# Mask additions spread between scalings, and the end of attention reordered in pairs, in a one-core two-block transformer kernel

## The chip, the cores and the metric

The kernel runs on one core of a Trainium2 chip. The metric is the device time of one execution in microseconds; the median of several runs is compared.

## What is computed

Two small transformer blocks run one after the other on 272 tokens (16 meta tokens and 256 others) of width 1024, in float32. The part that the change touches first is sparse attention in the first block. An index score chooses at most 64 keys for each query; the others are masked, and each head's logits get a bias:

```python
score = jnp.einsum('bqhs,bqh->bqs', jax.nn.relu(s_idx), wb)
top_val, top_idx = lax.top_k(score, n_sel)            # n_sel = 64
logits = jnp.einsum('bqhc,bqkc->bhqk', q_lat, c_sel) * ATT_HEAD_DIM ** -0.5
logits = logits + jnp.moveaxis(bias, -1, 1)           # one bias per head
p = jax.nn.softmax(logits, axis=-1)
u = jnp.einsum('bhqk,bqkc->bqhc', p, c_sel)
...
h = h + dsa_mixer(hn, ...)
h = h + swiglu(rmsnorm(h, norm_ffn[i]), ...)
```

The second block has latent attention (`mla_mixer`) in the same place of its second layer, followed by the same kind of residual addition, norm and gated feed-forward.

## The kernel before

All activations stand transposed in SBUF: `h[:, k, :]` is channel chunk k of 8 (128 channels on the partitions, 272 tokens along the row). Every float32 matrix product is made from three reduced-precision products: an operand is split into a high part (made by ScalarE: `uh` for weights, `xh` or `ah` for activations) and a rest (made by VectorE: `ul`, `xl`, `al`, each the value minus its high part). TensorE then multiplies high by high, high by rest and rest by high: 24 matmuls for a weight unit of 128 output channels (`product`, L489 to L491).

The weights come in slabs of 1 MB into 3 buffers `raw`. SyncE starts the load of slab s when the high parts and rests of slab s-3 are made. A slab gives two units. The calls `hi()` on ScalarE (L949) and `lo()` on VectorE (L1431) convert the next unit wherever they stand in the written order: `hi()` runs up to five units ahead of TensorE and `lo()` up to four. Each engine runs its instructions in the written order; semaphores tie the engines together. There are 4 PSUM banks for the linear products (`lin`) and 4 for the rest (`aux`), used in turn: a bank is filled again only when its last reader has signalled.

**The sparse attention's loop** runs over steps t. In step t TensorE multiplies the query unit of head t (t < 8) or a part of the output projection (`rows`, L531 to L533); then, for t-5, it multiplies the turned weights with the values (`attended`, L719), for t-4 it turns the normalised weights (`weights_turned`, L708: two transposes for the first 128 queries, three for the others), and for t-2 it makes the logits (`dsa_logits`, L697). VectorE in step t converts a unit (`lo()`), inverts the sums of head t-4 (L1773), copies a part of the turned weights (L1702), adds the masked bias to the logits of head t-3 (L1786), takes the two maxima (L1789), negates them (L1792) and scales the queries of head t out of PSUM (L1799). ScalarE takes the exponentials of head t-3 (L1233). GpSimd multiplies the exponentials of a head with the inverted sums, in two instructions (L2135); TensorE's transposes wait for them through `s_dp`.

The mask, once VectorE has made it (`d_acc`, L1769), is added to the biases of the 8 heads by GpSimd (L2129, 128x416 each, signal `s_bm`); L1786 for head hd waits for `s_bm` of hd+1. GpSimd makes all eight additions and then begins to scale.

**The end of both attentions** (`rows_h`, stages "d" and "m"). The output projection leaves its sums in four banks, two channel chunks a bank; the last matmul of bank j is of L533. For each chunk k VectorE adds the bank's half to `h` (L1467), ScalarE makes `xh` from it (L955) and VectorE then `xl` (L1437). TensorE needs `xh` and `xl` of chunk k in the k-th triple of matmuls of the feed-forward's first unit (unit 0, L489 to L491). GpSimd sums the squares of the chunks in `squares`: for k < 6 it squares (L2080) and adds (L2088); for k = 6, 7 VectorE squares (L1471), in `rows_h`, and GpSimd only adds. TensorE sums over the partitions after unit 1 (`total`, L555), ScalarE takes the root (L978), VectorE inverts it (L1447) and scales the finished banks (`gate`, L1443), by which bank 0 comes free for unit 4. Of the three `lo()` in `rows_h`, the first makes the rest of the feed-forward's unit 0, the second that of unit 1 and the third that of unit 2. The `hi()` ahead of the root on ScalarE is that of unit 6, whose slab is loaded into the buffer that unit 0 and 1 leave.

Of the kernel before, what the change touches and what calls it, by code (L numbers as in the profile page):

```python
# [9 lines left out]
ALU = mybir.AluOpType  # L10
# [4 lines left out]
T = 272  # L15
NM = 16
TQ = 256
D = 1024
KC = 8
# [83 lines left out]
def build(nc, A, out):  # L103
    ctx = ExitStack()
    with ctx:
        def sb(name, shape, dt=F32):
            return ctx.enter_context(nc.sbuf_tensor(name, shape, dt))

        def sem(name):
            return ctx.enter_context(nc.semaphore(name))  # L110

        h = sb("h", [P, KC, T])
# [16 lines left out]
        sqt = sb("sqt", [P, 2, T])  # L129
# [260 lines left out]
        def unit_hi(u):  # L390
            n = unit_n(u)
            return uh[u % NFIRST][:, 0:n * P].rearrange("p (k n) -> p k n", k=n)

        def unit_lo(u):
            n = unit_n(u)
            return ul[u % NUNIT][:, 0:n * P].rearrange("p (k n) -> p k n", k=n)

        def pieces(u):

            s, view, kc = units[u]  # L400
            src = view(raw[s % NRAW])
            if kc == "pad":
                return [(src, slice(0, src.shape[2]))]
            if kc == "heads":
                return [(src[:, g], slice(32 * g, 32 * g + 32)) for g in range(4)]
            return [(src, slice(0, P))]
# [8 lines left out]
        lin = Banks(psum[0:4], s_mm, {"D": sem("s_lin_dve"), "A": sem("s_lin_act"), "do": s_dout, "mo": s_mout})  # L415
# [11 lines left out]
        s_xh, s_xl, s_sq, s_ssq, s_rbc = (  # L427
            [sem(f"{n}{i}") for i in range(9)] for n in ("s_xh", "s_xl", "s_sq", "s_ssq", "s_rbc"))
# [988 lines left out]
        def _(e):  # L1417
            w = Seen(e)
# [3 lines left out]
            def lo():  # L1422

                nonlocal u
                if u == NU:
                    return
                w.wait_ge(s_hi, u + 1)
                if u >= NUNIT:
                    w.wait_ge(s_mm, unit_end[u - NUNIT])
                for a, cols in pieces(u):  # L1430
                    i = e.tensor_tensor(unit_lo(u)[:, :, cols], a, unit_hi(u)[:, :, cols].bitcast(F32), ALU.subtract)  # L1431
                i.then_inc(s_lo, 1)
                u += 1

            def x_lo(i, k, n0, g):
                w.wait_ge(s_xh[i], k + 1)
                e.scalar_tensor_tensor(xl[:, k, n0:T], h[:, k, n0:T], g, xh[:, k, n0:T].bitcast(F32), ALU.mult,  # L1437
                                       ALU.subtract).then_inc(s_xl[i], 1)
# [20 lines left out]

            def rows_h(stage, s_done, i, g):  # L1460
                lo()
                for k in range(KC):
                    if k:
                        x_lo(i, k - 1, NM, g(k - 1))
                    half = lin.bank((stage, "sum", k // 2))[:, (k % 2) * TQ:(k % 2) * TQ + TQ]
                    w.wait_ge(*lin.full((stage, "sum", k // 2)))
                    e.tensor_tensor(h[:, k, NM:T], h[:, k, NM:T], half, ALU.add).then_inc(s_done, 1)  # L1467
                    if k >= 6:
                        w.wait_ge(s_done, k + 1)
                        w.wait_ge(s_ssq[i], 2 * k - 3)  # L1470
                        e.tensor_tensor(sqt[:, k % 2, 0:TQ], h[:, k, NM:T], h[:, k, NM:T], ALU.mult).then_inc(s_sq[i], 1)  # L1471
                x_lo(i, KC - 1, NM, g(KC - 1))
                lo()
                lo()

            def wide(stage, parts, i, n0, x0, sq0, g, also=None):
# [284 lines left out]
            for t in range(14):  # L1761
# [8 lines left out]
                hd = t - 4  # L1770
# [7 lines left out]
                hd = t - 3  # L1778
# [15 lines left out]
                if t < 8:  # L1794
                    key = ("dq", t)
                    w.wait_ge(*lin.full(key))
                    if t >= 3:
                        w.wait_ge(*aux.full(("dL", t - 3)))
                    e.scalar_tensor_tensor(d_q[t % 3], lin.bank(key)[:, 0:TQ], 128.0 ** -0.5, rbc[:, NM:T], ALU.mult,  # L1799
                                           ALU.mult).then_inc(lin.empties(key, "D"), 1)  # L1800
            rows_h("d", s_dout, 3, lambda k: G(gcol["norm_ffn"] + 8 + k))

            def meta_square(t):
# [84 lines left out]
            for s in range(32):  # L1888
                hd, r = s // 8, s % 8
# [110 lines left out]
            for a in range(2):  # L2000
# [5 lines left out]
                for m, op in ((0, ALU.subtract), (2, ALU.add)):  # L2006
                    w.wait_ge(*lin.emptied(("mr", a, m // 2)))
                    for g in range(4):
                        rows_ = slice(32 * g, 32 * g + 32)
                        to = slice(64 * (g % 2) + 16 * m, 64 * (g % 2) + 16 * m + 32)  # L2010
                        i = e.tensor_tensor(m_qr[to, 2 * a + g // 2, :], tmp[m][rows_, 0:TQ], tmp[m + 1][rows_, 0:TQ], op)
                    i.then_inc(s_qr, 1)
            for t in range(13):
                lo()
                hd = t - 3
# [7 lines left out]
                hd = t - 2  # L2023
                if 0 <= hd < 8:
# [4 lines left out]
                    for b in range(2):  # L2029
# [4 lines left out]
                    e.tensor_scalar(m_stat[:, 1, 2 * hd:2 * hd + 2], m_stat[:, 0, 2 * hd:2 * hd + 2], -(192.0 ** -0.5),  # L2034
                                    None, ALU.mult).then_inc(s_mmax, 1)
            rows_h("m", s_mout, 7, lambda k: G(gcol["norm_ffn_g_2"] + 8 + k))


# [16 lines left out]
        def _(e):  # L2055
            w = Seen(e)

            def pad(u):

                if u >= NFIRST:  # L2060
                    w.wait_ge(s_mm, unit_end[u - NUNIT])
                e.memset(uh[u % NFIRST][:, :].bitcast(F32), 0.0).then_inc(s_pad, 1)
                e.memset(ul[u % NUNIT][:, :].bitcast(F32), 0.0).then_inc(s_pad, 1)

            def squares(i, stage, n0, between=None):

                total = ssq[0][:, 0:T - n0]
                w.wait_ge(*aux.full(("n", i - 1)))
                for k in range(KC):
                    src, sq = h[:, k, n0:T], sqt[:, k % 2, 0:T - n0]  # L2070
                    if k == 6 and between is not None:
                        pad(between)
                    if k < 6:
                        if stage in ("d", "m"):
                            w.wait_ge(s_dout if stage == "d" else s_mout, k + 1)
                        else:
                            w.wait_ge(*lin.emptied((stage, "o", k)))
                        if i == 4 and k >= 3:
                            w.wait_ge(s_both, k - 1)
                        e.tensor_tensor(sq if k else total, src, src, ALU.mult).then_inc(s_ssq[i], 1)  # L2080
                        w.wait_ge(s_ssq[i], 2 * k)
                    else:
                        w.wait_ge(s_sq[i], k - 5)
                        w.wait_ge(s_ssq[i], k + 5)
                    if i == 4 and k == 1:
                        w.wait_ge(s_both, 1)
                    if k:
                        e.tensor_tensor(total, total, sq, ALU.add).then_inc(s_ssq[i], 1)  # L2088
# [36 lines left out]
            e.tensor_tensor(total, total, sqt[:, 0, :], ALU.add).then_inc(s_dcs, 1)  # L2125
            w.wait_ge(s_bias, 16 * 2 * (P // NR))
            w.wait_ge(s_mask, 1)
            for hd in range(8):
                e.tensor_tensor(d_bias[:, hd, :], d_bias[:, hd, :], d_acc, ALU.add).then_inc(s_bm, 1)  # L2129
            for hd in range(8):  # L2130
                E = d_E[hd % 5]
                w.wait_ge(s_drc, hd + 1)
                for b in range(2):
                    Eb = E[:, KEYS[b]]
                    e.tensor_scalar(Eb, Eb, d_stat[:, 3, 2 * hd + b:2 * hd + b + 1], None, ALU.mult).then_inc(s_dp, 1)  # L2135
            squares(3, "d", NM)


# [177 lines left out]
```

## Time and profile before

| | |
|---|---|
| median of 3 runs | 1436.95 us (1436.87 to 1436.99) |
| the profiled execution's own time | 1435.41 us |
| its span, first to last instruction | 1433.5 us |
| TensorE busy | 1394.1 us, 97% |
| VectorE, ScalarE, GpSimd busy | 954.0, 691.2 and 275.5 us |
| mean granted TensorE clock | 0.991 of full speed |

All rows are of the one profiled execution. PE is TensorE (PEld its weight loads), DVE VectorE, ACT ScalarE, POOL GpSimd, SP SyncE. A matmul's recorded length includes its way through the array, so that back-to-back matmuls overlap in the records.

### The profile page before, as it was taken

The numbers are of one execution on the slowest core, as the hardware profiler recorded it, in microseconds if no ns is written. First come the engines' busy times: TensorE is split into PE (matmuls) and PEld (weight loads), VectorE is DVE, ScalarE is ACT, GpSimd is POOL, SyncE is SP. The second block draws the span as 40 slices with busy tenths as digits, with TensorE's granted clock in tenths as the row PEclk, the third lists the DMA queues.
The fourth block names the chain that finished last, engine by engine and source line by source line (L and its number), as shares of the span: only waits on it lengthen the run. The fifth ranks groups of instructions, "written<-read, shape, count | busy, mean of one in ns | idle before, by whom it ended". The sixth has DMA issues, their size and how long they took to land.

```text
span 1433.5 us, 26896 instructions
## 1 busy us (share of the span) xinstructions
PE 1394.1 (97%) x11056; PEld 1372.8 (96%) x11056; DVE 954.0 (67%) x1520; ACT 691.2 (48%) x1117; POOL 275.5 (19%) x273
## 2 busy tenths in 40 slices
PE   7999999999989999999999999999999999899998
PEld 7999999999989999999999999999999999899997
DVE  5668766656875767668566786766557775766653
ACT  5555544444644544444333564544444554544442
POOL 1024100022053000032233553000023302200021
PEclk9999999999999999999999999999999999999999
DMA  7424566555422655554444455555555552365551
GB/s 233 147 89 152 174 186 191 174 192 176 138 99 89 205 174 191 173 192 147 147 149 136 132 167 174 177 176 177 162 168 158 153 176 89 119 205 182 188 182 68
DMA packets 225489, 229.57 MB, mean 160 GB/s; under 512 B 13576, under 2 KB 218632, under 8 KB 225368
## 3 DMA queue, kind: packets, MB, share of 16 engines
q1 hardware_dynamic: 224432, 225.98, 48.9%
q10 hardware_dynamic: 936, 1.87, 0.6%
q8 instruction: 89, 1.46, 0.5%
q14 instruction: 32, 0.26, 0.1%
HBM read 226.51 MB, written 1.33 MB: 159 GB/s over the span
## 4 chain that ended last, share of the span: by engine, by line
PE 87%; DVE 7%; ACT 2%; issue 2%; POOL 2%; DMA 0%; POOLq 0%; DVEq 0%; ACTq 0%
PE ps L489 26%; PE ps L491 25%; PE ps L490 25%; DVE ul L1431 2%; PE ps L719 1%; PE ps L793 1%; PE ps L561 1%; DVE xl L1437 1%; POOL arena L2129 1%; PE ps L531 1%; PE ps L533 1%; PE ps L532 1%; ACT xh L955 1%; PE ps L708 1%; PE ps L555 1%
## 5 line engine op out<-in xcount | busy, mean ns | idle before, releaser
L949 ACT ACTIVATE uh<-raw 128x1024 fp32r<-128x1024 f32 (+4 forms) x455 | 449.1, 994 | 513.5 <-PE ps L491 468.7
L489 PE MATMUL ps<-xh,uh 128*128 128x272 f32 (+1 forms) x2160 | 631.3, 292 | 11.8 <-DVE xl L1437 8.0
L1431 DVE TENSOR_TENSOR ul<-raw,uh 128x1024 fp32r<-128x1024 f32 (+4 forms) x455 | 528.6, 1168 | 159.8 <-PE ps L491 129.8
L491 PE MATMUL ps<-xh,ul 128*128 128x272 f32 (+1 forms) x2160 | 619.9, 287 | 0.0
L490 PE MATMUL ps<-xl,uh 128*128 128x272 f32 (+1 forms) x2160 | 617.9, 286 | 0.0
L489 PEld LDWEIGHTS ps<-xh,uh 128*128 128x128 f32 x2160 | 409.2, 189 | 18.5 <-issue 12.1
L490 PEld LDWEIGHTS ps<-xl,uh 128*128 128x128 f32 x2160 | 408.8, 189 | 1.3
L491 PEld LDWEIGHTS ps<-xh,ul 128*128 128x128 f32 x2160 | 409.0, 189 | 0.0
L489 PE MATMUL ps<-ah,uh 128*128 128x272 f32 (+1 forms) x1104 | 319.7, 290 | 3.0 <-ACT ah L1077 2.7
L491 PE MATMUL ps<-ah,ul 128*128 128x272 f32 (+1 forms) x1104 | 315.1, 285 | 0.0
L490 PE MATMUL ps<-al,uh 128*128 128x272 f32 (+1 forms) x1104 | 314.9, 285 | 0.0
L1443 DVE TENSOR_TENSOR tmp<-ps,rbc 128x272 f32<-128x272 f32 (+1 forms) x224 | 96.6, 433 | 195.4 <-PE ps L491 192.5
L489 PEld LDWEIGHTS ps<-ah,uh 128*128 128x128 f32 x1104 | 208.5, 189 | 3.8 <-ACT ah L1077 2.9
L490 PEld LDWEIGHTS ps<-al,uh 128*128 128x128 f32 x1104 | 208.9, 189 | 0.5
L491 PEld LDWEIGHTS ps<-ah,ul 128*128 128x128 f32 x1104 | 208.5, 189 | 0.0
L2080 POOL TENSOR_TENSOR ssq<-h 128x272 f32<-128x272 f32 (+1 forms) x8 | 10.2, 1279 | 601.6 <-DVE h L1453 578.7
L2080 POOL TENSOR_TENSOR sqt<-h 128x272 f32<-128x272 f32 (+1 forms) x40 | 52.8, 1320 | 114.4 <-DVE h L1453 113.0
L2088 POOL TENSOR_TENSOR ssq<-ssq,sqt 128x272 f32<-128x272 f32 (+1 forms) x56 | 49.7, 888 | 60.5 <-DVE sqt L1458 54.4
L955 ACT ACTIVATE xh<-h,gains 128x272 fp32r<-128x272 f32 (+1 forms) x48 | 24.8, 517 | 65.4 <-DVE h L1453 48.0
L1000 ACT ACTIVATE ah<-tmp 128x272 fp32r<-128x272 f32 (+1 forms) x88 | 36.9, 420 | 12.9 <-DVE tmp L1503 12.9
L1437 DVE SCALAR_TENSOR_TENSOR xl<-h,gains,xh 128x272 fp32r<-128x272 f32 (+1 forms) x48 | 36.0, 751 | 7.7 <-ACT xh L955 6.9
L1503 DVE TENSOR_TENSOR tmp<-tmp 128x272 f32<-128x272 f32 (+1 forms) x88 | 38.1, 433 | 3.0
(253 smaller groups left out, 1168.7 us busy)
## 6 DMA issues: line engine op xcount, KB each, us to landing
raw<-in_ffn_w SPq DMA_DIRECT2D x60, 1024.0 KB, 5.2
raw<-in_ffn_w_in SPq DMA_DIRECT2D x44, 1024.0 KB, 5.2
raw<-in_ret_w_in SPq DMA_DIRECT2D x24, 1024.0 KB, 5.2
raw<-in_ffn_w_out SPq DMA_DIRECT2D x16, 1024.0 KB, 5.0
raw<-in_gla_w_in SPq DMA_DIRECT2D x12, 1024.0 KB, 6.1
raw<-in_ret_w_o SPq DMA_DIRECT2D x8, 1024.0 KB, 5.0
raw<-in_dsa_w_in SPq DMA_DIRECT2D x7, 1024.0 KB, 5.3
raw<-in_ffn_w_out SPq DMA_DIRECT2D x8, 768.0 KB, 4.3
```

What stands on the lines that cost most here:

```text
L489: e.matmul(ps[:, 0:n1 - n0], hi[:, k, :], x.hi[:, k0 + j, n0:n1], start=first and j == 0, stop=False)
L490: e.matmul(ps[:, 0:n1 - n0], hi[:, k, :], x.lo[:, k0 + j, n0:n1], start=False, stop=False)
L491: i = e.matmul(ps[:, 0:n1 - n0], lo[:, k, :], x.hi[:, k0 + j, n0:n1], start=False, stop=last and j == len(ks) - 1)
L949: i = e.activation(unit_hi(u)[:, :, cols], a, ACT.Copy)
L955: e.activation(xh[:, k, n0:T], h[:, k, n0:T], ACT.Copy, scale=g).then_inc(s_xh[i], 1)
L1000: e.activation(ah[:, c, n0:T], tmp[2 * c % 6][:, 0:n], ACT.Copy).then_inc(s_fh, 1)
L1431: i = e.tensor_tensor(unit_lo(u)[:, :, cols], a, unit_hi(u)[:, :, cols].bitcast(F32), ALU.subtract)
L1437: e.scalar_tensor_tensor(xl[:, k, n0:T], h[:, k, n0:T], g, xh[:, k, n0:T].bitcast(F32), ALU.mult, ALU.subtract).then_inc(s_xl[i], 1)
L1443: e.tensor_tensor(dst, lin.bank(key)[:, 0:T - n0], rbc[:, n0:T], ALU.mult).then_inc(lin.empties(key, "D"), 1)
L1503: e.tensor_tensor(t, t, tmp[(2 * c + 1) % 6][:, 0:n], ALU.mult).then_inc(s_prod, 1)
L2080: e.tensor_tensor(sq if k else total, src, src, ALU.mult).then_inc(s_ssq[i], 1)
L2088: e.tensor_tensor(total, total, sq, ALU.add).then_inc(s_ssq[i], 1)
```

## The change

Two reorderings; no arithmetic is added or taken away.

1. GpSimd adds the mask to the biases of heads 0, 1 and 2 first. Then, after it has scaled head hd, it adds the mask for head hd+3 (for hd < 5).
2. In `rows_h`, VectorE waits once a bank, adds both halves to `h`, and then makes both rests `xl`. The squares of chunks 6 and 7 are made after the second `lo()` and not between the additions and rests.

```diff
             def rows_h(stage, s_done, i, g):
                 lo()
-                for k in range(KC):
-                    if k:
-                        x_lo(i, k - 1, NM, g(k - 1))
-                    half = lin.bank((stage, "sum", k // 2))[:, (k % 2) * TQ:(k % 2) * TQ + TQ]
-                    w.wait_ge(*lin.full((stage, "sum", k // 2)))
-                    e.tensor_tensor(h[:, k, NM:T], h[:, k, NM:T], half, ALU.add).then_inc(s_done, 1)
-                    if k >= 6:
-                        w.wait_ge(s_done, k + 1)
-                        w.wait_ge(s_ssq[i], 2 * k - 3)
-                        e.tensor_tensor(sqt[:, k % 2, 0:TQ], h[:, k, NM:T], h[:, k, NM:T], ALU.mult).then_inc(s_sq[i], 1)
-                x_lo(i, KC - 1, NM, g(KC - 1))
+                for j in range(KC // 2):
+                    w.wait_ge(*lin.full((stage, "sum", j)))
+                    for k in (2 * j, 2 * j + 1):
+                        half = lin.bank((stage, "sum", j))[:, (k % 2) * TQ:(k % 2) * TQ + TQ]
+                        e.tensor_tensor(h[:, k, NM:T], h[:, k, NM:T], half, ALU.add).then_inc(s_done, 1)
+                    for k in (2 * j, 2 * j + 1):
+                        x_lo(i, k, NM, g(k))
                 lo()
+                for k in (6, 7):
+                    w.wait_ge(s_done, k + 1)
+                    w.wait_ge(s_ssq[i], 2 * k - 3)
+                    e.tensor_tensor(sqt[:, k % 2, 0:TQ], h[:, k, NM:T], h[:, k, NM:T], ALU.mult).then_inc(s_sq[i], 1)
                 lo()
...
             w.wait_ge(s_mask, 1)
-            for hd in range(8):
+
+            def hide(hd):
                 e.tensor_tensor(d_bias[:, hd, :], d_bias[:, hd, :], d_acc, ALU.add).then_inc(s_bm, 1)
+
+            for hd in range(3):
+                hide(hd)
             for hd in range(8):
                 E = d_E[hd % 5]
                 w.wait_ge(s_drc, hd + 1)
                 for b in range(2):
                     Eb = E[:, KEYS[b]]
                     e.tensor_scalar(Eb, Eb, d_stat[:, 3, 2 * hd + b:2 * hd + b + 1], None, ALU.mult).then_inc(s_dp, 1)
+                if hd < 5:
+                    hide(hd + 3)
             squares(3, "d", NM)
```

## Rows read from the trace of the kernel before

**Rows 1.** The page, part 1: busy time, share of the span, instructions.
```profile
PE 1394.1 (97%) x11056; PEld 1372.8 (96%) x11056; DVE 954.0 (67%) x1520; ACT 691.2 (48%) x1117; POOL 275.5 (19%) x273
```

**Rows 2.** TensorE's waits, 410 to 470 us: total, times, longest, in us.
```profile
PE ps L708 <- POOL arena L2135: 5.3, 2, 5.1
PE ps L489 <- DVE xl L1437: 3.4, 3, 1.4
```

**Rows 3.** Chain that ended last, 388 to 470 us: start, us, what.
```profile
397.60 11.24 POOL arena L2129 x8
...
411.53 0.88 PE ps L708 x3
412.41 1.39 PE ps L697 x4
...
417.19 1.12 PE ps L719 x10
...
418.85 0.71 PE ps L697 x4
...
422.40 1.11 PE ps L719 x10
...
469.88 0.55 PE ps L489
```

**Rows 4.** Granted clock: window, length, busy us (count) by engine, PEclk, DMA share, GB/s.
```profile
410.00:415.00 5.00, 4.13 (x16) 3.56 (x17) 1.70 (x5) 0.39 (x1) 2.94 (x4) 0.51 0.04 13
...
470.00:475.00 5.00, 5.00 (x30) 4.95 (x31) 3.71 (x4) 1.40 (x3) 0.06 (x1) 0.71 0.84 271
```

**Rows 5.** GpSimd in order of time, 386 to 456 us: start, us, instruction, [idle before].
```profile
408.83 4.11 POOL L2135 TENSOR_SCALAR arena<-arena 128x144 f32<-128x144 f32 x4
418.95 1.58 POOL L2135 TENSOR_SCALAR arena<-arena 128x144 f32<-128x144 f32 x2 [6.00 <-DVE arena L1773]
```

**Rows 6.** GpSimd in order of time, 401 to 402.5 us: the third mask addition.
```profile
400.66 2.06 POOL L2129 TENSOR_TENSOR arena<-arena 128x416 f32<-128x416 f32 x1
```

**Rows 7.** VectorE in order of time, 386 to 425 us.
```profile
403.00 0.79 DVE L1792 TENSOR_SCALAR arena<-arena 128x2 f32<-128x2 f32 x1
...
404.04 1.85 DVE L1431 TENSOR_TENSOR ul<-raw,uh 128x1024 fp32r<-128x1024 f32 x1
...
420.99 0.17 DVE L1792 TENSOR_SCALAR arena<-arena 128x2 f32<-128x2 f32 x1
```

**Rows 8.** VectorE in order of time, 448 to 482 us.
```profile
456.07 0.42 DVE L1467 TENSOR_TENSOR h<-h,ps 128x256 f32<-128x256 f32 x1 [0.70 <-PE ps L533]
457.07 0.49 DVE L1437 SCALAR_TENSOR_TENSOR xl<-h,gains,xh 128x256 fp32r<-128x256 f32 x1 [0.58 <-ACT xh L955]
...
465.67 1.04 DVE L1437 SCALAR_TENSOR_TENSOR xl<-h,gains,xh 128x256 fp32r<-128x256 f32 x1
...
468.52 4.62 DVE L1431 TENSOR_TENSOR ul<-raw,uh 128x1024 fp32r<-128x1024 f32 x4
...
479.64 0.75 DVE L1443 TENSOR_TENSOR tmp<-ps,rbc 128x256 f32<-128x256 f32 x2
```

**Rows 9.** GpSimd in order of time, 448 to 482 us.
```profile
459.51 0.61 POOL L2080 TENSOR_TENSOR sqt<-h 128x256 f32<-128x256 f32 x1
...
465.71 0.72 POOL L2088 TENSOR_TENSOR ssq<-ssq,sqt 128x256 f32<-128x256 f32 x1 [0.36 <-DVE sqt L1471]
```

**Rows 10.** ScalarE in order of time, 448 to 482 us: the high parts of unit 6.
```profile
474.97 1.06 ACT L949 ACTIVATE uh<-raw 128x1024 fp32r<-128x1024 f32 x1 [3.60 <-DMA raw<-in_ffn_w_in]
```

**Rows 11.** TensorE in order of time, 450 to 476 us: last matmul of bank 3.
```profile
462.12 0.28 PE L533 MATMUL ps<-ah,ul 128*128 128x256 f32 x1
```

**Rows 12.** TensorE in order of time, 479.4 to 480.9 us: first matmul of unit 4.
```profile
480.22 0.28 PE L489 MATMUL ps<-xh,uh 128*128 128x256 f32 x1
```

**Rows 13.** The same two places in stage "m": TensorE in order of time, 1216 to 1242 us.
```profile
1230.09 0.28 PE L533 MATMUL ps<-ah,ul 128*128 128x256 f32 x1
...
1237.84 0.55 PE L489 MATMUL ps<-xh,uh 128*128 128x256 f32 x1 [0.54 <-DVE ul L1431]
```

## The prediction, as it was recorded before the changed kernel was run

> **What bounds the kernel now.** I read the page first: TensorE is busy for 97% of the span [rows 1]. So a change saves time only where TensorE waits, or where its clock is down because it waited. TensorE's waits near the two edits come next [rows 2]: 5.3 us for GpSimd's scalings, of which one wait is 5.1 us, and 3.4 us for the rests `xl` (stage "d"; "m" looks the same). Third, the chain of work that ended last, for what released each wait [rows 3]. From 397.60 to 408.84 us it is GpSimd's eight mask additions, then two scalings, then the transposes of head 0 at 411.53. From 456 us on it passes to and fro between VectorE and ScalarE, chunk by chunk, and TensorE starts unit 1 of the feed-forward at 469.88. Last, the granted clock [rows 4]: 0.51 in 410 to 415 and 0.71 in 470 to 475, so each of the two waits is followed by some microseconds at 1.2 GHz where the rest of the stage runs at 2.4 GHz. The logits' four matmuls show it: 1.39 us at 412.41, 0.71 us at 418.85 [rows 3].
>
> All sums are differences within this one execution (1433.5 us of span, 1435.41 us own time). The median of the runs is 1.5 us above it, and I take the saving off the median.
>
> **Part A, the masks.** Nothing is removed: eight additions and sixteen scalings remain on GpSimd, and no DMA or wait is added. Only five additions move behind scalings.
>
> The first three additions fall as now. The third begins at 400.66 and lasts 2.06 us [rows 6], so it ends at 402.7. Until then VectorE sees what it sees now. After that GpSimd is free, where now additions four to eight run to 408.84. VectorE's little negation at 403.00 lasts 0.79 us beside them and 0.17 us at 420.99, where GpSimd is idle; the `lo()` at 404.04 lasts 1.85 us, against 4.62 / 4 = 1.15 us [rows 7, 8]. I count on both becoming short: 0.6 and 0.65 us. The `lo()` then runs from 403.4 to 404.6, the sums of head 0 are inverted there (ScalarE's exponentials begin at the negation's end and move with it), and GpSimd can begin to scale head 0 at 404.8. A pair of scalings lasts 1.58 us [rows 5], so the second ends at 406.4 and TensorE's second group of transposes starts at 406.5 instead of 411.53: 5.0 us.
>
> Behind it TensorE does three transposes, the logits of head 2 and unit 5, and comes to `attended` of head 0 at 417.19, all of it partly at the low clock. At the high clock the logits take 0.71 us, a unit 422.40 - 418.85 - 0.71 = 2.84 us, and the three transposes half of their 0.88, 0.44 us. `attended` then begins at 406.5 + 0.44 + 0.71 + 2.84 = 410.5, against 417.19: **6.7 us**. TensorE is left with a wait of under 1 us, and I assume that the clock stays up.
>
> Does something else come late next? From `attended` on the steps are TensorE's: one every 422.40 - 417.19 = 5.2 us. GpSimd has per step 1.58 us of scaling and one addition of 11.24 / 8 = 1.4 us in the mean [rows 3], 2.06 us beside a `lo()` [rows 6]: at most 3.6 of 5.2 us. The tightest is head 1. Behind the scaling of head 0 the addition for head 3 (406.4 on) and VectorE's next `lo()` want the same time; I let VectorE wait 0.8 us for it, so it ends at 408.4, and head 1 is scaled from 408.6 to 410.2. TensorE wants it after `attended`, at 411.6: 1.4 us to spare. The addition for head hd+3 is wanted by L1786 about two steps later, 10 us. Should TensorE not wait for the first scalings at all, A is 7.4 us; should only the 5.0 us come and the clock stay low as now, 5.0 us.
>
> **Part B, the ends of "d" and "m".** Now one chunk follows the other: `h`, 1.00 us later `xl` (456.07 to 457.07 [rows 8]), then the next `h`. That is 1.4 us a chunk, 2.8 us a bank, while TensorE fills a bank with 18 matmuls in 18 x 2.84 / 24 = 2.13 us. Bank 3 is full at 462.12 + 0.28 = 462.4 [rows 11]. The second `lo()` begins at 468.52, ends 1.2 us later and lets TensorE into unit 1 at 469.88 [rows 3, 8].
>
> In the new order ScalarE makes `xh` of one chunk while VectorE adds the other. If nothing hinders, a bank takes 1.00 + 2 x 0.49 = 1.98 us, less than TensorE's 2.13. Then `h` of chunk 6 comes at 462.4, `xl` of 6 at 463.4, `xl` of 7 ends at 464.4, the `lo()` at 465.55, and TensorE starts unit 1 at 465.7: 4.2 us earlier. The two squares of VectorE lie behind this `lo()`.
>
> But GpSimd sums squares all that time. The `xl` at 465.67 lasts 1.04 us against 0.49 alone, beside an addition that started at 465.71 [rows 8, 9]: 0.55 us of waiting, and in effect it starts 0.5 us after the addition did. From that row an addition of 0.72 us holds VectorE off for 0.5 us, and I take 0.4 us of the square's 0.61 [rows 9]. An `xl` in turn holds off GpSimd for some 0.4 us. If they alternate, a bank costs 2 x (0.5 + 0.4 + 0.4) = 2.6 us, so VectorE falls behind by up to 0.5 us a bank. Walked through with its first bank free, it starts chunk 6 some 0.55 us late and loses some 0.35 us more in bank 3. That puts the `lo()`'s end at 466.45 and unit 1 at 466.6: **3.3 us** earlier.
>
> On what a busy GpSimd costs VectorE there is a rule in the Trainium skill, "SBUF — State Buffer", section "SBUF: two separate sides": the pair of ports that both use is an exclusive lock, held for the whole instruction, and the other fully blocks. The rows agree that one waits for the other, but show 0.5 us of a 0.72 us instruction. By the rule to the letter each of some five `xl` would wait 0.2 us longer, B would be about 2.3 us a stage and the time about 1425.5 us.
>
> TensorE would gain 1.4 us more from a clock that stays up through unit 1 (15 matmuls at twice 0.12 us at present). It can't keep it: unit 4 needs bank 0, which the scaling at 479.64 frees at 480.06, and unit 4 starts at 480.22 [rows 8, 12]: 0.2 us of slack. That scaling ends a chain of fixed length: second `lo()` done (469.7), slab loaded into the buffer that comes free, high parts of unit 6 at 474.97 [rows 10], table load, root, reciprocal. It moves with the `lo()`, 3.3 us, and TensorE would be there 4.7 us earlier. So it waits there for about 1.2 us, and B is 3.3 + 0.2 = **3.5 us**. The new place of the squares costs nothing here: GpSimd's last addition would end near 469.4, when TensorE reaches `total` (466.6 + 2.84), and up to 1.2 us of delay goes into that same wait. In "m" the last matmul of bank 3 and the first of unit 1 lie 1237.84 - 1230.09 = 7.75 us apart, in "d" 469.88 - 462.12 = 7.76 [rows 13, 3, 11], so B counts twice.
>
> **Sum:** 6.7 + 2 x 3.5 = 13.7 us; 1436.95 - 13.7 = **1423.2 us** (-0.95%). Bounds: most 7.4 + 2 x 5.0 = 17.4 (unhindered `xl`, and part of the clock's gain as well): 1419.5. Least 5.0 + 2 x 2.3 = 9.6: 1427.4.
>
> **Rivals.**
> *The clock's gain is kept.* If the chain to unit 4 gets shorter too (a load with less beside it), B is 3.3 + 1.4 = 4.7 us a stage and the time 1436.95 - 6.7 - 9.4 = 1420.9 us. For it: the load of unit 6's slab has a second one beside it now. Against: it starts with the same `lo()`. 0.14.
> *The end of attention gives nothing.* VectorE and GpSimd block each other so much that a bank costs 2.8 us as now, or the chain to unit 4 doesn't move. Then only A is left: 1430.2 us. Against it: even then two squares of 0.4 to 0.5 us and their blocked `xl` leave the path. 0.08.
> *The interleaved additions come into TensorE's path.* If each of the five delays its next scaling so far that TensorE waits the mean addition of 1.4 us: 7.0 us back, 1430.2 us. Against it: 1.4 us to spare at head 1, more later. 0.06. The port rule cited above would push this way; the spare time covers it.
> *Slower.* The long waits become several short ones (near 406, 465, 476 us), and if the clock then stays low, each matmul costs 0.12 us more. It would take (13.7 + 2.9) / 0.12, about 140 matmuls, six units more at 1.2 GHz, to come out slower by 0.2%, say 1441 us. For it: both present drops follow waits. Against: the remaining waits sum to less. 0.03.
> *As forecast,* 0.69.
>
> A measurement of this kernel tells 0.2% (2.9 us) from no change. The range of 8 in 10 is 1419.5 to 1428.0, which takes in the forecast and the first rival and leaves out 0.17. Faster by more than 0.2%: 0.95; within: 0.02; slower: 0.03.
>
> **What would show it.** Step A: the first L2135 starts near 405, with three L2129 ahead and five between; TensorE's 5.1 us wait is under 1 us; the clock in 405 to 415 is near 1. Step B: from bank 3's last matmul to unit 1 some 4.5 instead of 7.8 us; `xl` of 0.5 to 1 us; a new TensorE wait of about 1 us for the scaling L1443 ahead of unit 4. The forecast is wrong if the low clock comes back in either place, if L1786 waits for a mask, or if the load ahead of unit 6 lasts otherwise than now.

## The result, and the profile after

The changed kernel takes 1421.1 us (median of 4 runs, 1420.71 to 1421.77), the kernel before beside it 1436.91 us: a ratio of 0.9897, 95% interval 0.9885 to 0.9909. Run once more, on another occasion (`e3_after_again`), it is 1421.45 us against 1435.59 us, ratio 0.9905 (0.989 to 0.9921). The forecast was 1423.2 us, a ratio of 0.9905. The two profiled executions, 1435.41 and 1421.77 us, have spans of 1433.5 and 1419.9 us: 13.6 us, where the working of the forecast had 13.7.

**The masks.** GpSimd in order of time, 386 to 456 us of the changed kernel (L2130 is the mask addition, L2139 the scaling), to be held against [rows 5, 6]:

```profile
397.45 5.12 POOL L2130 TENSOR_TENSOR arena<-arena 128x416 f32<-128x416 f32 x3 [36.57 <-DVE arena L1769]
404.65 1.59 POOL L2139 TENSOR_SCALAR arena<-arena 128x144 f32<-128x144 f32 x2 [2.08 <-DVE arena L1773]
406.21 2.12 POOL L2130 TENSOR_TENSOR arena<-arena 128x416 f32<-128x416 f32 x1
408.30 1.59 POOL L2139 TENSOR_SCALAR arena<-arena 128x144 f32<-128x144 f32 x2
```

Head 0 is scaled from 404.65 on, not from 408.83. In the gap of 2.08 us ahead of it GpSimd now waits for VectorE (L1773). VectorE in the same time (compare [rows 7]):

```profile
402.85 0.17 DVE L1792 TENSOR_SCALAR arena<-arena 128x2 f32<-128x2 f32 x1
...
403.26 1.21 DVE L1431 TENSOR_TENSOR ul<-raw,uh 128x1024 fp32r<-128x1024 f32 x1
404.40 0.15 DVE L1773 RECIPROCAL arena<-arena 128x2 f32<-128x2 f32 x1
```

Both instructions that were long beside GpSimd's fourth and fifth additions are short: 0.17 instead of 0.79 us, 1.21 instead of 1.85 us. The moved additions lengthen the same small negation in later steps (L1792 at 414.26 lasts 0.63 us), but VectorE then waits for TensorE anyway, for 0.82 us ahead of its next instruction. No L1786 waits for a mask: VectorE has no wait for GpSimd between 395 and 450 us.

TensorE's waits from 395 to 480 us (compare [rows 2]):

```profile
PE ps L489 <- DVE tmp L1443: 0.9, 1, 0.9
PE ps L489 <- DVE ul L1431: 0.5, 1, 0.5
PE ps L708 <- POOL arena L2139: 0.5, 1, 0.5
PE ps L531 <- DVE al L1709: 0.4, 1, 0.4
PE ps L489 <- DVE xl L1437: 0.3, 1, 0.3
```

The long wait of 5.1 us is down to 0.5 us, the 3.4 us for the rests are down to 0.3 us, and one wait is new: 0.9 us for the scaling L1443, ahead of unit 4. The granted clock (columns as in [rows 4]):

```profile
405.00:410.00 5.00, 4.43 (x35) 3.96 (x34) 4.30 (x12) 2.79 (x10) 5.00 (x6) 1.00 0.66 213
410.00:415.00 5.00, 5.00 (x43) 4.92 (x43) 4.29 (x9) 2.28 (x6) 3.57 (x4) 1.00 0.32 92
...
460.00:465.00 5.00, 5.00 (x41) 4.93 (x41) 5.00 (x6) 1.51 (x3) 4.15 (x3) 1.00 0.66 212
```

It is 1.00 in 410 to 415 us, where it was 0.51, and 1.00 after the end of attention too, where it was 0.71.

**The ends of attention.** VectorE in order of time, 444 to 480 us of the changed kernel (compare [rows 8]; L1466 is the addition to `h`, L1473 the square):

```profile
454.81 1.42 DVE L1437 SCALAR_TENSOR_TENSOR xl<-h,gains,xh 128x256 fp32r<-128x256 f32 x2 [0.25 <-ACT xh L955]
456.15 0.74 DVE L1466 TENSOR_TENSOR h<-h,ps 128x256 f32<-128x256 f32 x2
457.14 1.42 DVE L1437 SCALAR_TENSOR_TENSOR xl<-h,gains,xh 128x256 fp32r<-128x256 f32 x2 [0.25 <-ACT xh L955]
458.48 1.21 DVE L1431 TENSOR_TENSOR ul<-raw,uh 128x1024 fp32r<-128x1024 f32 x1
459.62 0.75 DVE L1473 TENSOR_TENSOR sqt<-h 128x256 f32<-128x256 f32 x2
```

A bank now takes 458.48 - 456.15 = 2.3 us instead of 2.9. The forecast had 2.0 us for a bank that nothing hinders. The lines of L1437 show the difference: two rests last 1.42 us beside GpSimd, where two last 0.9 us without it (`e7_gpsimd_late` below). TensorE's rows at the same place (compare [rows 3, 11, 12]) are the last matmul of bank 3 and the first ones of unit 1 and unit 4:

```profile
455.46 0.28 PE L533 MATMUL ps<-ah,ul 128*128 128x256 f32 x1
...
459.84 0.36 PE L489 MATMUL ps<-xh,uh 128*128 128x256 f32 x1 [0.55 <-DVE ul L1431]
...
469.94 0.39 PE L489 MATMUL ps<-xh,uh 128*128 128x256 f32 x1 [0.87 <-DVE tmp L1443]
```

Unit 1 follows bank 3 after 4.38 us (before: 7.76), unit 4 after 14.48 us (before: 18.10). In stage "m" unit 1 follows after 4.46 us (before: 7.75).

The chain of work that ended last, between unit 1 and unit 4 (start, us, what), is the chain that the forecast put there:

```profile
458.48 1.22 DVE ul L1431
...
459.77 5.00 DMA raw<-in_ffn_w_in
...
464.79 1.06 ACT uh L949
...
465.87 1.28 ACT L978
...
467.17 0.48 ACT rbc L978
...
467.67 1.76 DVE rbc L1447
...
469.46 0.43 DVE tmp L1443
...
469.94 0.39 PE ps L489
```

The second `lo()` ends at 459.69, the slab load starts at once and lands 5.0 us later, then come the high parts of unit 6, a table load, the root, the reciprocal and the scaling. TensorE isn't on it for 10 us.

### The profile page after: what moved, and what is told of

Its sections match the earlier page's. It is cut to its first block, busy times and chain, and to the rows that moved or that the text cites. A ratio compares the mean times of both kernels' runs of the same rounds, so it can differ in the third digit from the quotient of the medians.

```text
span 1419.9 us, 26896 instructions
## 1 busy us (share of the span) xinstructions
PE 1389.9 (98%) x11056; PEld 1368.7 (96%) x11056; DVE 955.2 (67%) x1520; ACT 690.2 (49%) x1117; POOL 277.5 (20%) x273
## 4 chain that ended last, share of the span: by engine, by line
PE 86%; DVE 8%; ACT 2%; issue 2%; DMA 1%; POOL 1%; POOLq 0%; DVEq 0%; ACTq 0%; SPq 0%
PE ps L489 25%; PE ps L491 25%; PE ps L490 25%; DVE ul L1431 2%; PE ps L719 1%; PE ps L793 1%; PE ps L561 1%; DVE xl L1437 1%; PE ps L531 1%; PE ps L533 1%; PE ps L532 1%; PE ps L783 1%; PE ps L708 1%; PE ps L629 1%; PE ps L555 1%
## 5 line engine op out<-in xcount | busy, mean ns | idle before, releaser
L1443 DVE TENSOR_TENSOR tmp<-ps,rbc 128x272 f32<-128x272 f32 (+1 forms) x224 | 96.8, 434 | 195.3 <-PE ps L491 192.4
L1453 DVE TENSOR_TENSOR h<-h,ps 128x272 f32<-128x272 f32 (+1 forms) x48 | 20.6, 429 | 28.9 <-PE ps L491 28.7
```

Of the source, the lines that this page charges most:

```text
L1443: e.tensor_tensor(dst, lin.bank(key)[:, 0:T - n0], rbc[:, n0:T], ALU.mult).then_inc(lin.empties(key, "D"), 1)
L1453: e.tensor_tensor(h[:, k, n0:T], h[:, k, n0:T], lin.bank(key)[:, 0:T - n0], ALU.add).then_inc(lin.empties(key, "D"), 1)
```

## The experiments

### Each part alone, and the changed kernel again

`e1_masks_only` is the kernel before with the reordered masks alone (part A), `e2_rows_only` is the kernel before with the reordered ends of attention alone (part B).

> Only the mask additions are moved; the end of attention is as before. My theory (the two parts are separate and each is worth what the profile of the changed kernel shows): 6.7 us less than before, near 1430.2 us; TensorE waits 0.5 us for the scaling of head 0 and 3.4 us for the rests of h, as before. Rival (the parts overlap: what part A brings forward, the slab loads or the end of attention take back, or part A is worth more than the profiled pair of runs tells): under 5 us or over 8 us.

> Only the two ends of attention are reordered; the masks are as before. My theory: 2 x 3.5 = 7.0 us less than before, near 1429.9 us; TensorE keeps the 5.1 us wait for the scalings of head 0, and shows two new waits of about 1 us ahead of unit 4 of the two feed-forwards. Rival (a part of the saving needs part A, or the measured 15.8 us between the medians come from here): 9 us or more, or under 5 us.

> The changed kernel once more, as the yardstick for the other three. The profiled pair of executions differs by 13.6 us, the medians by 15.8 us. If the difference of the medians was scatter between executions, this comes out between 13.5 and 15 us less than before; if something outside the profiled execution is saved, 15.5 us or more.

| | median us (runs) | ratio to before, interval | profiled span |
|---|---|---|---|
| masks only | 1428.22 (1427.69 to 1428.79) | 0.9949, 0.9936 to 0.9961 | 1426.9 |
| ends only | 1428.37 (1427.63 to 1428.92) | 0.9950, 0.9937 to 0.9962 | 1426.8 |
| both | 1421.45 (1420.84 to 1423.52) | 0.9905, 0.9890 to 0.9921 | 1419.3 |

The kernel before was 1435.59 us beside them. By spans the parts are worth 6.6 and 6.7 us against 1433.5, and 14.2 together: they add up within 1 us. By medians it is 7.4, 7.2 and 14.1 us. Each profile shows the other part's waits as they were: with the masks only TensorE waits 0.5 us for the scaling and 3.4 us for the rests, with the ends only 5.0 us for the scaling at its longest, and it has the new waits for L1443 (2.3 us in two). So the two parts are separate, and both rivals fall.

The 14.1 us lie in the band that I had set for scatter (13.5 to 15 us). The kernel before spreads more from run to run (1433.82 to 1437.68) than the others, and its mean granted clock goes with its time: 0.993 in the fastest of the nine runs, 0.988 in the slowest. The 15.8 us of the first comparison lie within that scatter.

### The slab of unit 6

In `e4_root_first` every feed-forward takes the root before it waits for the slab:

```diff
                 for j in range(FC // 2):
                     for t in range(4):
-                        hi()
                         if j == 0 and t == 2:
                             root(("n", 2 * f + 1), float(D), eps6, rbc[:, n0:T])
+                        hi()
+                        if j == 0 and t == 2:
                             silu(0)
```

> The changed kernel, but in every feed-forward ScalarE takes the root of the norm before and not after the high parts of unit 6, so that the scaling that frees bank 0 no longer waits for the slab of unit 6. My theory (unit 4 is held by the chain slab load, high parts, root, reciprocal, scaling): the waits of 0.9 and 1.05 us ahead of unit 4 in the feed-forwards after both attentions go, and the kernel is 2 us faster than the changed one, the other two feed-forwards giving little. Rival (what is saved there comes back at unit 5 or 6, since the high parts of unit 6 come later): the changed kernel's time within 0.5 us.

Measured: 1418.56 us (1417.99 to 1419.05), 2.9 us below the changed kernel on the same occasion, ratio to before 0.9881 (0.9868 to 0.9895). ScalarE, 455 to 475 us:

```profile
460.48 1.28 ACT L978 ACT_TABLE_LOAD   x1
462.60 0.48 ACT L978 ACTIVATE rbc<-ps,small 128x256 f32<-128x256 f32 x1 [0.83 <-PE ps L555]
463.95 1.06 ACT L949 ACTIVATE uh<-raw 128x1024 fp32r<-128x1024 f32 x1 [0.88 <-DMA raw<-in_ffn_w_in]
```

The root is now released by TensorE's `total` (L555) and the slab is waited for behind it. TensorE's two waits ahead of unit 4, 1.9 us together, are gone. Counted at TensorE's weight loads, which begin ahead of the matmuls in this trace, they are longer; first the changed kernel, then this one:

```profile
PEld ps L489 <- DVE tmp L1443: 3.3, 4, 1.3
```

```profile
PEld ps L489 <- DVE tmp L1444: 0.9, 2, 0.5
```

Of the four waits for L1443 the two of 1.1 and 1.3 us in the feed-forwards after both attentions are gone, 2.4 us; the two others, 0.9 us together near the kernel's start, are as before. Unit 4 follows bank 3 after 13.52 us in "d" and 13.50 us in "m", where the changed kernel has 14.48 and 14.71: 2.2 us in all, and unit 6 is not later for it (19.20 instead of 20.27 us after bank 3 in "d"), so the rival falls. The chain through the slab held just these two places, and what the clock had to give after the ends of attention was waiting behind it. The 0.5 to 0.7 us that are left of the 2.9 are within the scatter of single executions.

### The place of the squares, and the pairs

`e5_squares_moved_only` has the changed masks, the old order chunk by chunk, and the squares behind the second `lo()`. `e6_squares_inside` has the pairs, but the squares inside the last one:

```diff
                         e.tensor_tensor(h[:, k, NM:T], h[:, k, NM:T], half, ALU.add).then_inc(s_done, 1)
+                    if j == 3:
+                        for k in (6, 7):
+                            w.wait_ge(s_done, k + 1)
+                            w.wait_ge(s_ssq[i], 2 * k - 3)
+                            e.tensor_tensor(sqt[:, k % 2, 0:TQ], h[:, k, NM:T], h[:, k, NM:T], ALU.mult).then_inc(s_sq[i], 1)
                     for k in (2 * j, 2 * j + 1):
                         x_lo(i, k, NM, g(k))
                 lo()
-                for k in (6, 7):
...
                 lo()
```

> The changed masks; in the ends of attention the old order chunk by chunk, but the two squares of VectorE after the second rest of the weights. It tells how much of part B is the squares' place and how much the pairs. My theory: a chunk still takes 1.4 us, the squares and the rest that waits behind GpSimd leave the path: unit 1 begins 1.1 us sooner after bank 3 than before the change (6.7 instead of 7.8 us), so the time is about 2 x 2.2 = 4.5 us above the changed kernel, near 1425.8 us. Rival (the squares' place is most of part B): within 2 us of the changed kernel.

> The changed kernel, but both squares stand in the last pair, between the additions to h and the rests xl. My theory: VectorE then waits in the last bank for GpSimd's sums of chunks 4 and 5, which end near 456.8 and 458.3 us in the changed kernel, before it can make the rests; unit 1 begins 1.1 us later, about 2 us in all: near 1423.4 us. Rival (the place of the squares costs nothing once the chunks go in pairs): the changed kernel's time within 0.7 us.

Measured: 1427.67 us (1426.14 to 1428.0) and 1426.29 us (1424.47 to 1428.27), with the kernel before at 1435.92 us; forecast were 1425.8 and 1423.4. The profiled spans are 1424.3 and 1426.3 us. Both rivals fall: the two are 6.2 and 4.8 us above the repeated changed kernel, where the rivals had up to 2 and 0.7 us. The place of unit 1 is as I worked it out in the first case: in `e5_squares_moved_only` it follows bank 3 after 462.25 - 455.62 = 6.63 us (forecast 6.7). In `e6_squares_inside` it is 462.11 - 455.76 = 6.35 us, 2.0 us later than with the squares outside, where I had 1.1. Its VectorE rows say why:

```profile
457.22 0.75 DVE L1471 TENSOR_TENSOR sqt<-h 128x256 f32<-128x256 f32 x1
458.66 0.43 DVE L1471 TENSOR_TENSOR sqt<-h 128x256 f32<-128x256 f32 x1 [0.69 <-POOL ssq L2089]
459.00 1.82 DVE L1437 SCALAR_TENSOR_TENSOR xl<-h,gains,xh 128x256 fp32r<-128x256 f32 x2
```

The second square waits 0.69 us for GpSimd's sum of chunk 5, and then both rests are held off by GpSimd's next additions: 1.82 us for two.

The rest of the difference is the clock. Windows of `e5_squares_moved_only`, then of `e6_squares_inside`:

```profile
460.00:465.00 5.00, 4.05 (x19) 3.61 (x18) 4.52 (x6) 4.24 (x5) 2.34 (x3) 0.54 0.34 95
465.00:470.00 5.00, 5.00 (x34) 4.95 (x34) 3.49 (x3) 2.33 (x2) 1.78 (x2) 0.78 0.88 284
```

```profile
460.00:465.00 5.00, 4.75 (x19) 4.28 (x20) 5.00 (x5) 1.70 (x2) 2.29 (x2) 0.52 0.34 107
465.00:470.00 5.00, 5.00 (x35) 4.95 (x34) 1.59 (x2) 2.49 (x3) 0.00 (x0) 0.80 0.97 316
```

Mean clocks of 0.54 and 0.52 against 1.00 in the changed kernel: with only one of the two edits TensorE waits 2.3 and 1.9 us for rests ahead of unit 1 and then runs unit 1 mostly at 1.2 GHz. From unit 1 to `total` it takes 5.14 and 5.11 us, where the changed kernel takes 2.89. There is no wait for L1443 left in either kernel: TensorE now comes later than the chain to unit 4. From bank 3's last matmul to the two units, in us, one profiled execution each:

| | unit 1, "d" and "m" | unit 4, "d" and "m" |
|---|---|---|
| before | 7.76, 7.75 | 18.10, 18.10 |
| squares moved only | 6.63, 6.70 | 17.88, 17.26 |
| pairs only (squares inside) | 6.35, 6.44 | 17.56, 17.83 |
| both | 4.38, 4.46 | 14.48, 14.71 |
| both, root first | 4.48, 4.47 | 13.52, 13.50 |

At unit 1 in "d" the squares alone are worth 1.1 us, the pairs alone 1.4 us, and both 3.4 us, more than their sum: inside the pairs the squares cost 2.0 us, as VectorE reaches them before GpSimd's sums are there. At unit 4, where it counts, the single edits have left only 0.2 and 0.5 us of this and both edits together 3.6 us. The 3.4 us at unit 4 in "d" between the squares alone and the changed kernel are 2.25 us of unit 1's place and 2.25 us of low clock in unit 1, less 1.1 us by which the changed kernel takes longer from `total` to unit 4, mostly its wait for the scaling.

What the clock takes is not the same each time. In "m" of `e5_squares_moved_only` unit 1 takes 4.46 us behind the same 2.3 us of waits for rests. The five runs of `e6_squares_inside` go from 1424.47 us (mean clock 0.996) to 1428.27 us (0.992), and the profiled one is at the slow end, while that of `e5_squares_moved_only` is the fastest of its five. Which of the two single edits is worth more is therefore not shown; that both together are worth more than the sum shows in the medians as well: 0.9 and 2.3 us beyond the masks alone, and 6.8 us for both.

### Does GpSimd hold VectorE off?

In `e7_gpsimd_late` GpSimd waits for all eight sums before it squares:

```diff
-                            w.wait_ge(s_dout if stage == "d" else s_mout, k + 1)
+                            w.wait_ge(s_dout if stage == "d" else s_mout, KC)
```

> The changed kernel, but GpSimd begins its squares in both ends of attention only when all eight sums are in h, so that it is idle beside the pairs. It is read by its profile. My theory (GpSimd's instructions hold VectorE off): the pairs of rests last 0.9 us instead of 1.24 to 1.42 us, and unit 1 begins 3.5 to 3.6 us after bank 3's last matmul instead of 4.4; the sum of the squares then comes 3 to 5 us late for the norm, so the whole is slower than the changed kernel, near 1428 us. Rival (the rests are long for another reason, such as ScalarE's pace): the pairs last as long as in the changed kernel and unit 1 begins 4.4 us after bank 3.

VectorE's last two banks in this kernel:

```profile
454.39 0.75 DVE L1466 TENSOR_TENSOR h<-h,ps 128x256 f32<-128x256 f32 x2 [0.24 <-PE ps L533]
455.39 0.88 DVE L1437 SCALAR_TENSOR_TENSOR xl<-h,gains,xh 128x256 fp32r<-128x256 f32 x2 [0.25 <-ACT xh L955]
456.50 0.75 DVE L1466 TENSOR_TENSOR h<-h,ps 128x256 f32<-128x256 f32 x2 [0.23 <-PE ps L533]
457.50 1.54 DVE L1437 SCALAR_TENSOR_TENSOR xl<-h,gains,xh 128x256 fp32r<-128x256 f32 x2 [0.25 <-ACT xh L955]
458.97 1.75 DVE L1431 TENSOR_TENSOR ul<-raw,uh 128x1024 fp32r<-128x1024 f32 x1
```

With GpSimd idle two rests last 0.88 us and a bank 2.11 us, TensorE's pace (VectorE waits 0.24 us for it). The last pair and the `lo()`, beside which GpSimd has started, last 1.54 and 1.75 us. ScalarE's pace is the same in both kernels (VectorE waits 0.25 us for `xh` in each pair). So the theory holds and the rival falls. The forecast for unit 1 failed for the same reason: I had left out that GpSimd starts exactly at the last pair, and unit 1 came 4.68 us after bank 3. TensorE then waits 5.1 us at each `total`, and the one run was 1436.07 us, 8 us above my figure. Unit 4 is 21.43 us behind bank 3 in "d", 6.95 us later than in the changed kernel: 0.3 us at unit 1 and the wait of 5.1 us, less the 0.9 us for the scaling that are gone, and 2.4 us more, nearly all of it in the two units behind `total`, with the clock at 0.57 in 470 to 475 us. In "m" it is 6.84 us. The two make up 13.8 of the 14.6 us that this run is above the repeated changed kernel.

### How many masks ahead

`e8_two_ahead`, `e9_five_ahead` and `e10_six_ahead` change only the number, for five:

```diff
-            for hd in range(3):
+            for hd in range(5):
                 hide(hd)
...
-                if hd < 5:
-                    hide(hd + 3)
+                if hd < 3:
+                    hide(hd + 5)
```

> The changed kernel with two masks ahead instead of three: the third addition moves behind the scaling of head 0. My theory: VectorE's rest of the weights at 399.9 us, 1.77 us long beside the third addition, gets 0.3 to 0.5 us shorter, head 0 is scaled that much sooner and TensorE's wait of 0.5 us for it is about gone: 0.4 us faster by the profile, too little for the times to tell. Rival (the third addition comes too late for the logits of head 2): VectorE waits for a mask, and TensorE's steps behind it come up to 1 us later.

> The changed kernel with five masks added before the first scaling instead of three. It splits part A into the wait itself and the clock that falls after it, and is read by the stretch from the mask (L1769) to the values' product of head 0 (L719): 20.1 us before the change, 13.5 us with three ahead. My theory (each addition delays the scalings of head 0 by one addition, and the clock falls only after the longest of these waits): the scalings come 1.2 us later than with three ahead, TensorE waits under 2 us, the clock stays at 2.4 GHz and the stretch is 14.7 us. Rival (the clock falls after any longer wait): 1.6 us more, 16.3 us.

> The same with six masks ahead. My theory: the scalings of head 0 come 2.3 us later than with three ahead, TensorE waits about 3 us; the stretch from L1769 to L719 is 15.8 us if the clock stays at 2.4 GHz and 17.4 us if it falls to 1.2 GHz. I expect it to fall here at the latest partly, since before the change 5.1 us of waiting were followed by the low clock: 16 to 17.4 us. Rival (the low clock needs nearly the full 5 us): 15.8 us.

From the mask (L1769) to the second group of transposes of head 0 and to its values' product (L719), in us, and TensorE's waits between:

| masks ahead (one profiled execution each) | to the transposes | to L719 | between the two | TensorE waited |
|---|---|---|---|---|
| 2 | 9.45 | 13.36 | 3.91 | 0.5 |
| 3 | 9.46 | 13.37 | 3.91 | 0.5 |
| 5 | 10.72 | 16.17 | 5.45 | 1.8 |
| 6 | 11.45 | 16.86 | 5.41 | 2.6 |
| 8 (before) | 14.45 | 19.95 | 5.50 | 5.3 |

The fourth column is the same work each time, without a wait in it, and it has two values: 3.9 us, and 5.4 to 5.5 us. With five ahead the clock falls already (0.75 in 405 to 410, 0.91 in 410 to 415), after waits of 1.3 and 0.5 us:

```profile
405.00:410.00 5.00, 3.31 (x15) 2.90 (x16) 4.48 (x13) 2.31 (x7) 4.64 (x5) 0.75 0.65 213
410.00:415.00 5.00, 5.00 (x40) 4.92 (x39) 2.80 (x7) 2.73 (x7) 2.16 (x3) 0.91 0.00 0
```

So the rival was right for five (16.2 us; it said 16.3, my theory 14.7), and six came within its range. Of the 6.6 us of part A the wait is 14.45 - 9.46 = 5.0 us and the clock 1.6 us, and the 1.6 us come whole once the waits are down to 0.5 us. All eight profiles with this single wait of 0.5 us (those of the other experiments with three ahead among them) show a clock of 1.00 in 405 to 415 us; that five and six ahead always lose it rests on one execution each. The one time of each (1424.05 and 1425.38 us) has the kernel before beside it at 1438.0 us and isn't used.

Two ahead gives nothing: 1421.56 us (1420.56 to 1422.52), ratio to before 0.9900 (0.9885 to 0.9915), where the changed kernel had 0.9897 and 0.9905 on its two occasions. TensorE's wait stays 0.5 us, and the `lo()` that I wanted to shorten still lasts 1.77 us, so it is GpSimd's second addition that lengthens it, not the third. The rival's wait does appear, 0.52 us of VectorE for the mask of head 2, but it comes out of VectorE's idle time:

```profile
400.51 1.77 DVE L1431 TENSOR_TENSOR ul<-raw,uh 128x1024 fp32r<-128x1024 f32 x1
...
409.07 0.59 DVE L1786 TENSOR_TENSOR arena<-ps,arena 128x416 f32<-128x416 f32 x1 [0.52 <-POOL arena L2130]
```

## Why the prediction was right

The time lay in the range and the mechanisms were those forecast. These are the terms against what the profiled pair shows:

- Part A, 6.7 us: measured 6.6. The 5.0 us of waiting and the clock's part behind it are separated by the experiments on masks ahead. That the clock would stay up with a wait of under 1 us was assumed; no row of the kernel before told how short a wait has to be. The wait was 0.5 us and the clock stayed up; behind 1.8 us in two waits (`e9_five_ahead`) it fell and the same work took 1.5 us more. So this assumption was in part lucky. The step on head 1 had the order wrong: VectorE's `lo()` went first (1.22 us) and GpSimd's addition behind it lasted 2.12 us. Head 1 was scaled from 408.30, I had 408.6, and it made no difference to TensorE. The spare time of the first moved addition was overstated: it ended at 408.33, and L1786 of head 3 began at 412.96, 4.6 us later and not 10.
- Part B up to unit 1, 3.3 us a stage: measured 3.4 and 3.3. GpSimd's hold on VectorE, estimated from a single row of 1.04 us, is confirmed by `e7_gpsimd_late`. Without it the sum would have had 4.2. The bank that this estimate gave was too long (2.6 us, measured 2.2 to 2.3), as a pair of rests is held off once, for 0.54 us. The walk to the last bank came out close even so: chunk 6 started 0.4 us late and bank 3 lost 0.35 us, forecast 0.55 and 0.35.
- The slack of 0.2 us at unit 4 and the chain of fixed length: 18.10 - 14.48 = 3.6 us in "d" and 18.10 - 14.71 = 3.4 us in "m", forecast 3.5. From the load's start to the high parts of unit 6 it is 5.02 us in "d", before 5.17, so this length was nearly fixed. TensorE waited 0.9 and 1.05 us there, forecast about 1.2. `e4_root_first` shows the chain by taking the slab out of it.
- The squares' new place costs nothing: GpSimd's two last additions end at 462.65, and `total` starts at 462.73, as early as TensorE could be there. This was closer than I would have liked; the two take 2.54 us beside VectorE's `lo()`.
- The whole: 13.7 us forecast, 13.6 us between the profiled executions. The forecast time was 2.1 us too high, which is within the scatter of the kernel before: on the four occasions it was 1436.91, 1435.59 and 1435.92 us (medians) and 1438.0 us (one run). That the sum came within 0.1 us of the profiled pair is luck, as single executions of the kernel before differ by almost 4 us.

Of the rivals, "the clock's gain is kept" described a gain that is there but locked behind the slab of unit 6: the experiment that unlocks it reaches 1418.56 us. "The end of attention gives nothing" is refuted by `e2_rows_only`, 7.2 us below the kernel before. "The interleaved additions come into TensorE's path" did not happen with three ahead. "Slower" did not happen either, but its mechanism exists: in `e5_squares_moved_only` three waits of 0.7 to 0.8 us were followed by the low clock. The rule in the Trainium skill, "SBUF — State Buffer", section "SBUF: two separate sides", says that the loser blocks for the whole instruction. The runs show the blocking, and 3.4 us a stage where, by the estimate in the prediction, the rule to the letter would have left about 2.3. Where my expectations failed in `e5_squares_moved_only`, `e6_squares_inside`, `e7_gpsimd_late` and `e9_five_ahead`, it was each time the clock: I priced a wait by its length and not by what TensorE ran at behind it, and in `e6_squares_inside` and `e7_gpsimd_late` also VectorE's instructions that GpSimd lengthened. In `e8_two_ahead` I had the wrong addition holding up the `lo()`.

## What to carry to other kernels

A helper engine that prepares data for all items before it serves the first one puts the whole preparation on the path of the first item; what matters is how far ahead it has to be, and here two or three of eight are enough, and five are too many. When two engines hand a chunk to and fro, give each two chunks at a time, and move what a third engine paces (here the squares) behind the work that the bottleneck waits for: the two edits together gave more than their sum, because squares inside the pairs have to wait for the third engine, and because either edit alone left waits behind which the clock fell. After such a gain follow the chain to the next wait: a slab wait that stood in ScalarE's order ahead of the norm's root had taken 2.2 to 2.9 us of the gain back.

## What was not expected of the hardware

- Waits of 1.3 and 0.5 us of TensorE, 0.5 us of work between them, were followed by granted clocks of 0.75 and 0.91, and the same work took 5.45 instead of 3.91 us; after a single wait of 0.5 us it did not (eight profiles of eight). After 5.3 us of waiting the loss was about the same, 1.6 us. Behind 2.3 us of waits for rests in three pieces unit 1 took 5.14 us at one place and 4.46 us at another.
- An instruction of 2 elements a partition on VectorE (L1792) lasted 0.79 us beside a GpSimd addition and 0.17 us without one.
